# Cached K turned in 32x32 blocks on VectorE, scores a batch at a time with 32x32 tiles, and other places for the pages of K and V

## What is computed

```python
def moba_sample(q, k_new, v_new, cache_k, cache_v, page_table, layer):
    k_past = cache_k[layer, page_table].reshape(B, past, H, HD)
    kmean = jnp.mean(k_past.reshape(B, n_full, MOBA_BLOCK, H, HD), axis=2)
    idx, ok = moba_select(q, kmean, n_full)            # the 3 best of 8 blocks of 256 tokens
    s_sel = einsum('bqhd,bhqnkd->bhqnk', q, k_sel) * scale
    s_own = einsum('bqhd,bkhd->bhqk', q, k_own) * scale, causal
    return sparse_softmax_attend(s_sel, v_sel, s_own, v_own)
```

## Time and profile before

| | before |
|---|---|
| runs (us) | 977.66, 979.59, 980.74; median 979.59 |
| profiled execution, its own time | 983.45 us |
| its span | 981.3 us |
| TensorE busy / weight load | 919.1 us (94%) / 798.8 us |
| VectorE, ScalarE, GpSimd busy | 545.9, 359.5, 28.1 us |
| attention over the cache | from 446 to 670 us of the span |
| DMA | 199.93 MB, mean 204 GB/s |

### The profile page before, as it was taken

One profiled execution on the slowest core, in us unless ns is written; L12 is line 12 of the kernel. 1 busy time (PEld: TensorE's weight loads), 2 busy tenths in 40 slices (PEclk: granted clock), 3 DMA queues, 4 the chain that ended last, 5 costly groups with the idle time before them and its releaser, 6 DMA issues.

```text
span 981.3 us, 17319 instructions
## 1 busy us (share of the span) xinstructions
PE 919.1 (94%) x6991; PEld 798.8 (81%) x6991; DVE 545.9 (56%) x839; ACT 359.5 (37%) x509; POOL 28.1 (3%) x34
## 2 busy tenths in 40 slices
PE   6999999999999899999878999859899999989997
PEld 2588888988999599996665877548779999989994
DVE  0545444454655677785843538443666765554655
ACT  1424322232442534454642426240333232323433
POOL 0000000000000000000000000001200000000000
PEclk9999999998999999999999889877999999999999
DMA  9899889886456744448858998996416465534511
GB/s 329 258 299 258 240 244 257 245 235 169 127 152 191 256 129 145 144 153 268 297 190 325 324 325 310 356 343 199 125 39 167 133 163 139 145 89 122 155 50 53
DMA packets 214885, 199.93 MB, mean 204 GB/s; under 512 B 9569, under 2 KB 161261, under 8 KB 214678
## 3 DMA queue, kind: packets, MB, share of 16 engines
q1 hardware_dynamic: 213412, 194.99, 64.8%
q0 software_dynamic: 704, 2.49, 0.7%
q10 hardware_dynamic: 690, 1.35, 0.4%
HBM read 195.00 MB, written 3.80 MB: 203 GB/s over the span
## 4 chain that ended last, share of the span: by engine, by line
PE 83%; DVE 6%; ACT 3%; SPq 3%; issue 2%; DMA 2%; ACTq 0%; DVEq 0%
PE B L691 20%; PE B L692 19%; PE B L696 19%; PE B L751 4%; PE B L887 3%; PE B L898 2%; SPq L619 2%; PE B L936 2%; PE B L775 2%; PE B L760 2%; PE B L791 2%; DMA ring<-in_cache_v 1%; PE B L1017 1%; PE B L717 1%; PE B L712 1%
## 5 line engine op out<-in xcount | busy, mean ns | idle before, releaser
L691 PE MATMUL B<-Hh,wh 128*128 128x320 f32 x912 | 274.2, 314 | 0.6 <-issue 0.6
L692 PE MATMUL B<-Hl,wh 128*128 128x320 f32 x912 | 270.5, 310 | 0.0
L1595 DVE TENSOR_TENSOR wl<-raw,wh 128x2048 fp32r<-128x2048 f32 x90 | 207.3, 2305 | 94.3 <-ACT wh L1240 94.0
L1240 ACT ACTIVATE wh<-raw 128x2048 fp32r<-128x2048 f32 x90 | 172.3, 1914 | 150.3 <-PE B L696 117.6
L691 PEld LDWEIGHTS B<-Hh,wh 128*128 128x128 f32 x912 | 172.4, 189 | 10.7 <-issue 10.0
L692 PEld LDWEIGHTS B<-Hl,wh 128*128 128x128 f32 x912 | 172.4, 189 | 0.3
L696 PE MATMUL B<-Hh,wl 128*128 128x320 f32 x912 | 152.8, 310 | 0.0
L696 PEld LDWEIGHTS B<-Hh,wl 128*128 128x128 f32 x912 | 139.1, 189 | 0.0
L691 PE MATMUL B<-Gh,wh 128*128 128x320 f32 x352 | 107.1, 317 | 2.5 <-DVE Gl L1721 2.5
L692 PE MATMUL B<-Gl,wh 128*128 128x320 f32 x352 | 106.7, 316 | 0.0
L1240 ACT ACTIVATE sg<-B 128x320 f32<-128x320 f32 x46 | 20.1, 438 | 210.1 <-PE B L696 195.7
(11 more groups left out here) (246 smaller groups left out, 951.8 us busy)
## 6 DMA issues: line engine op xcount, KB each, us to landing
raw<-in_w_ffn_in SPq DMA_DIRECT2D x88, 512.0 KB, 6.2
raw<-in_w_ada SPq DMA_DIRECT2D x72, 512.0 KB, 4.9
ring<-in_cache_k SPq DMA_DIRECT2D x108, 256.0 KB, 5.3
ring<-in_cache_v SPq DMA_DIRECT2D x84, 256.0 KB, 5.0
raw<-in_w_ffn_out SPq DMA_DIRECT2D x32, 384.0 KB, 3.6
raw<-in_w_mix_in SPq DMA_DIRECT2D x24, 512.0 KB, 4.7
raw<-in_w_ffn_out SPq DMA_DIRECT2D x32, 320.0 KB, 4.3
M<-in_cache_v SPq DMA_DIRECT2D x16, 256.0 KB, 4.5
```

The lines of the kernel that those rows point to most:

```text
L691: pe.matmul(out, w, xh[k], start=start and k == 0, stop=False)
L692: pe.matmul(out, w, xl[k], start=False, stop=False)
L1240: return act.activation(out, in_, func, **kw)
L1595: dve.tensor_tensor(wl[:, wbuf(n), :], raw_view(n), f32(wh[:, wbuf(n), :]), ALU.subtract).then_inc(lo_ready, 1)
```

## The change

- **K.** A group of K is turned in place on VectorE: `dve.transpose` over 128 x 2048 turns each block of 32x32 (`turn_keys` moves from TensorE to VectorE; 4 a batch, counted by `k_turned`). The TensorE transposes, `kT`, `keys_act` and `keys_dve` go.
- **Scores.** `scores(i, bi)` handles a batch: for each x (of four blocks of 32 features within a head pair), row group a (32 token rows) and head pair c a matmul with 32 partitions, 32 output rows and 512 columns (16 pages x 32), into S4[32c.., a, :], four banks where B0 to B3 were. x sums up, and so do the two samples. `s_out` counts once a batch.
- **Queries.** `turn_queries` copies each batch's `Qz` on TensorE into the four row groups (16 matmuls with 32 columns of the identity), `queries_out` on ScalarE puts them in `Qs`. The first two stand behind slot 7 of the projection. `Qz` moves into constants that are dead by then; its clearing and filling come later.
- **Reading scores.** `scores_out` reads 256 columns (a block) an instruction, reordering them, and its accumulator gives the block's sum (`gate`): 8 instructions a pair after the second batch. `block_max` takes maxima from `prob` in two instructions.
- **Order.** `values(i, 1)` and `pick_heads(i)` run in pair i + 1's part, before its probabilities are turned. All of `probs_act` is ScalarE's. Pieces of `mix` stand at points 0 to 14, four points a pair; mix(13) before the probabilities of pair 1 are turned, mix(14) and mix(18) between `values(i, 0)` and `scores(i + 1, 0)`.
- **Places.** Eight places lie in `ring` (now over raw, wh and wl). K(0, first batch) has 0 to 3, K(0, second) 4 to 7 (6 and 7 are `prob` and `PT` afterwards), every later batch of K 0 to 3. V has 4, 5 and `IN_H`, from pair 1 on one in M; without `IN_H` from pair 2; for the last pair also 0 to 3, two more in M and one in W. V of pair 0 goes to IN_H, 4, 5, IN_H again. SP waits for `s_out` of the whole batch before it loads over K.
- **Queue order.** K(0) both batches, one V group; then for each pair K(i + 1, 0), V(i, 0), K(i + 1, 1), V(i, 1). MO and MO + 1, both now into W, before the sixth and the fourth last group.
- `BANK` hands out banks 5 to 7; OB becomes bank 4.

```diff
-GROUPS = RING // 4
+GROUPS = 8
...
-AT_POINT = {0: 0, 1: 1, 3: 2, 4: 3, 5: 4, 6: 5, 8: 6, 9: 12, 10: 13, 11: 14, 13: 15, 14: 16, 15: 17, 16: 18, 18: 19}
+AT_POINT = {x: x if x <= 6 else x + 5 for x in range(15)}
...
+PAGE_GROUPS = key_groups(0, 0) + key_groups(0, 1) + value_groups(0, 0)[:1]
+for _i in range(NPAIR):
     if _i + 1 < NPAIR:
-        PAGE_GROUPS += [("k", _i + 1, 2, bi) for bi in range(2)]
-    PAGE_GROUPS += [("v", _i, g, 1) for g in range(4)]
...
+        PAGE_GROUPS += key_groups(_i + 1, 0)
+    PAGE_GROUPS += value_groups(_i, 0)[1 if _i == 0 else 0:]
     if _i + 1 < NPAIR:
...
+        PAGE_GROUPS += key_groups(_i + 1, 1)
+    PAGE_GROUPS += value_groups(_i, 1)
...
+    for n, (kind, i, g, bi) in enumerate(PAGE_GROUPS):
+        if kind == "k":
+            b = g + 4 if (i, bi) == (0, 1) else g
+        else:
+            open_ = [b for b in FIRST_IN if FIRST_IN[b] <= n <= LAST_IN.get(b, n)]
+            b = min(open_, key=lambda b: USE_AT[PAGE_GROUPS[last[b]]] if b in last else -1)
...
                 if kind == "k":
-                    sp.wait_ge(tp_filled, FILL_AT[("k", i, g, bi, 3)] + 1)
+                    sp.wait_ge(s_out, batch(i, bi) + 1)
...
+                elif b >= 4:
+                    sp.wait_ge(used, [n for n in (MI + 10, MI + 11) if wbuf(n) == b % 2][0] + 1)
...
+            def turn_queries(i, bi):
+
+                bank = turn_bank(("q", i, bi))
+                if i == 0:
+                    pe.wait_ge(q_ready, 4)
+                for x in range(4):
+                    for q in range(4):
+                        m = pe.matmul(bank[32 * q:32 * q + 32, P * x:P * (x + 1)], ident[:, 32 * x:32 * x + 32],
+                                      Qz[:, 2 * i + bi, :, :].rearrange("p c r -> p (c r)"), start=True, stop=True)
+                m.then_inc(tp_filled, 1)
+
+            def scores(i, bi):
+
+                if bi == 0 and i >= 1:
+                    pe.wait_ge(s_act, 2 * i)
+                wait_act(("q", i, bi))
+                pe.wait_ge(k_turned, 4 * batch(i, bi) + 4)
+                b = min(BUF[GROUP_AT[("k", i, g, bi)]] for g in range(4))
+                for x in range(4):
+                    for a in range(4):
+                        for c in range(HP):
+                            f = P * c + 32 * x
+                            m = pe.matmul(S4[32 * c:32 * c + 32, a, :].rearrange("r (p j) -> r p j", p=NPAGE),
+                                          Qs[32 * a:32 * a + 32, bi, x, c, :],
+                                          ring[32 * a:32 * a + 32, 4 * b:4 * b + NPAGE, f:f + 32],
+                                          start=(bi == 0 and x == 0), stop=(bi == 1 and x == 3))
+                m.then_inc(s_out, 1)
...
             for i in range(NPAIR):
-                m0 = 5 * i + 3
+                m0 = 4 * i + 3
+                point(m0)
+                if i:
+                    values(i - 1, 1)
+                    pick_heads(i - 1)
+                point(m0 + 1)
+                turn_probs(i)
+                values(i, 0)
                 if i + 1 < NPAIR:
...
+                    point(m0 + 2)
+                    scores(i + 1, 0)
+                    if i + 2 < NPAIR:
+                        turn_queries(i + 2, 0)
+                    point(m0 + 3)
+                    own_scores(i + 1)
+                    scores(i + 1, 1)
+                    if i + 2 < NPAIR:
+                        turn_queries(i + 2, 1)
+            values(NPAIR - 1, 1)
+            pick_heads(NPAIR - 1)
...
+                for m in range(4):
+                    n = 4 * s + m
+                    last = act_(prob[:, BLK * n:BLK * (n + 1)].rearrange("p (q a j) -> p a q j", q=2, a=4),
+                                S4[:, :, 64 * n:64 * n + 64].rearrange("p a (q j) -> p a q j", q=2),
+                                accum_out=gate[:, n:n + 1])
+                last.then_inc(s_act, 1)
...
+            def turn_keys(i, bi, lo, hi):
+
+                for key in key_groups(i, bi)[lo:hi]:
+                    n = GROUP_AT[key]
+                    b = BUF[n]
+                    dve.wait_ge(page_landed[b], 64 * TURN_IN[n])
+                    v = ring[:, 4 * b:4 * b + 4, :].rearrange("p j f -> p (j f)")
+                    dve.transpose(out=v, in_=v).then_inc(k_turned, 1)
...
+                if n >= 10:
+                    turn_keys(0, 0, 2 * (n - 10), 2 * (n - 10) + 2)
...
+            turn_keys(0, 1, 0, 2)
+            own(0)
             point(1)
...
+            turn_keys(0, 1, 2, 4)
             for i in range(NPAIR):
-                m0 = 5 * i + 3
...
+                m0 = 4 * i + 3
+                block_max(i, 0)
+                block_max(i, 1)
+                choose(i)
+                if i == 0:
+                    point(2)
+                point(m0)
+                if i:
+                    own_heads(i - 1)
                     out_low(i - 1)
                 if i + 1 < NPAIR:
...
+                    turn_keys(i + 1, 0, 0, 2)
+                point(m0 + 1)
                 if i + 1 < NPAIR:
...
+                    turn_keys(i + 1, 0, 2, 4)
+                totals(i)
+                probs_dve(i, 4)
+                if i + 1 < NPAIR:
                     point(m0 + 2)
...
                     point(m0 + 3)
...
+                    own(i + 1)
+                    turn_keys(i + 1, 1, 0, 4)
```

More of the change, by code:

```diff
@@ L135, in mix_fills, with key_groups, value_groups, batch @@
     return fills
-def key_fills(i, j):
-    return [("k", i, j, bi, p) for bi in range(2) for p in range(4)]
-PAGE_GROUPS = [("k", 0, j, bi) for j in range(4) for bi in range(2)]
+def key_groups(i, bi):
+    return [("k", i, g, bi) for g in ((2, 3, 0, 1) if i == 0 and bi == 0 else range(4))]
+def value_groups(i, bi):
+    return [("v", i, g, bi) for g in range(4)]
+def batch(i, bi):
+    return 2 * i + bi
 GAPS = [[] for _ in range(12)]
@@ L151 @@
     GAPS[6 + _lv] += mix_fills(7 + _lv)
+GAPS[7] += [("q", 0, bi) for bi in range(2)]
 GAPS[8] += [("nv", t) for t in range(3)]
@@ L166 @@
 for _i in range(NPAIR):
-    _m = 5 * _i + 3
-    if _i + 1 < NPAIR:
[L169 to L173, removed]
+    _m = 4 * _i + 3
+    FILLS += point_fills(_m)
+    if _i:
+        USE += value_groups(_i - 1, 1)
+        FILLS += [("pick", _i - 1)]
+    FILLS += point_fills(_m + 1) + [("p", _i, q) for q in range(5)]
@@ L184 @@
+    PAGE_GROUPS += value_groups(_i, 1)
 GROUP_AT = {key: n for n, key in enumerate(PAGE_GROUPS)}
+USE_AT = {key: n for n, key in enumerate(USE)}
 FILL_AT = {key: n for n, key in enumerate(FILLS)}
-IN_RING, IN_H, IN_M, IN_W = range(GROUPS), GROUPS, GROUPS + 1, GROUPS + 2
-BEGIN_AT = {GROUP_AT[("v", 1, 0, 0)]: IN_M, GROUP_AT[("v", 2, 0, 0)]: IN_W}
-LAST_IN = {IN_H: GROUP_AT[("v", 2, 3, 0)], IN_M: GROUP_AT[("k", 3, 3, 1)], IN_W: GROUP_AT[("v", 3, 0, 0)]}
-def place_groups():
[L193 to L199, removed]
+IN_H, IN_M, IN_M1, IN_M2, IN_W2 = range(GROUPS, GROUPS + 5)
@@ L266, in shape_constants @@
     parts["cos"], parts["sin"] = cos, sin
+    reset = np.ones((P, N))
+    reset[:, [0] + [S + T * b for b in range(NB)]] = 0.0
+    parts["reset"] = reset
     q = p[:, None]
@@ L1360, in probs_act @@
             def probs_act(i):
-                for q in (2, 3):
+                for q in range(4):
                     wait_fill(("p", i, q))
@@ L1480, in _ @@
                     level_exps(1)
+                if n == 7:
+                    queries_out(0, 0)
+                    queries_out(0, 1)
                 if n == 8:
@@ L1548, in _ @@
+            for b in (4, 5):
+                _, vi, vg, vb = PAGE_GROUPS[LAST_GROUP[b]]
+                act.wait_ge(v_used, v_index(vi, vb, vg) + 1)
+                high(At(MO + b - 4))
+            out_high(NPAIR - 1)
             for k in range(4):
@@ L2142, in _ @@
+            low(At(MO))
+            own_heads(NPAIR - 1)
+            out_low(NPAIR - 1)
+            low(At(MO + 1))
             dve.wait_ge(stored, STORED_MIX * 16)
```

315 lines of the change are left out of this document (94 added, 221 removed).

## The result

The changed kernel takes 1042.05 us (median, 1038.04 to 1051.06), the kernel before 980.13 beside it: ratio 1.0642, 95% interval 1.0595 to 1.0689, so 62 us more. A repeat in another series gave 1.0635 (1.058 to 1.069). I had predicted 1001.0, in the range 968 to 1034: slower as forecast, but by three times as much. The profiled execution took 1044.89 us, its span is 1042.9.

The account below looks back on a forecast made before the run. The in-order load queue bounds the cache attention: transfers plus rests, 63 us replacing 45. Projection start 678.9, plus 1.8, 2.7 and 8.0, gives 691.4 against 670.0: +21.4 on 979.6, so 1001.0 us, range 968 to 1034.

Parts of the forecast that it names:

- No change: Rival: half the faster case's savings hidden, or turns at their low bound and the clock holds; 983 to 984 us, chance 0.11.
- the faster first pair: Rival: VectorE and ScalarE steps overlap, so the first pair's rests of 9.6 and 16.9 go; 966.5 us, chance 0.20.
- slow turns: Rival: VectorE's turn of a K group is slower than its landing; 1015 us at 3.3 each, 1039 at twice; chance 0.08.
- the tile rival: Rival: row tiles share TensorE's array in the scores; 42, 57 or 120 ns a record give 1015, 1031, 1092; chance 0.11.
- The sum of the queue's walk: Attention over the cache: 168.0 us of transfers plus 63.0 of queue rests put the last V at 674.1 us.
- the allowances of 12.5 us: Added after the walk: 1.8 us for turning queries, 2.7 for loading out_gla_sample, 8.0 for TensorE's clock.
- (b): Scores on TensorE: 128 records of 32x32 tiles at 28 ns, 3.6 us a batch, 29 in all.
- (d): VectorE's 32 turns of K groups: 2.3 us each, below the 2.7 us in which a group lands.
- K(i+1, second batch) waits for scores(i+1, first): Load queue: K reuses four places, so once a pair it rests until scores end; 9.4, 16.0 and 9.1 us.
- the rival in which these three rests vanish: K takes other places, so rests before its second batches go, 34.5 us; 966.5 us, chance shared with the 0.20 faster case.
- In a batch only the last turn shows: VectorE's turns, 2.3 us each, hide behind the 2.7 us landings of K groups, except a batch's last.
- The allowance of 8 us for the clock: TensorE idles before five score batches and restarts at a lower clock: 1.6 us each, 8.0 in all.

Follow-up runs that it names:

- e9: Changed kernel with the next pair's first scores moved between the third and fourth group of values(i, first half) on TensorE; 1016.55 us, ratio 1.0361.
- e1: Changed kernel with the next pair's first scores moved before values(i, first half) on TensorE; 1039.15 us, ratio 1.0609.
- e2: Changed kernel with unread products added on TensorE before five score batches (18, 45, 52) to keep its clock up; 1065.16 us, ratio 1.0842.
- e5: Changed kernel with fewer unread products added before five score batches (11, 27, 30) to keep TensorE's clock up; 1040.26 us, ratio 1.0611.
- e15: Same kernel as e5, measured again in more rounds; 1041.49 us, ratio 1.0626.

## Why the prediction was wrong, point by point

**Right.** The bound is the queue, and its rests make the time: +61.5 us of rests for +62. The turn, 2.3 us forecast, 2.297 measured; the Trainium skill's rate ("Vector Engine (DVE) Microarchitecture Reference", § 3.8), one element per cycle and lane, gave an estimate of some 2.1, a little under the 2.297 of the trace. The transposes saved on TensorE show nowhere in the time, though no run takes them alone. In this stage SP waits longest at the score line (71.6 us), and before each second batch TensorE waits 13 to 18 us for turns, where I had 10 to 13. No change, the faster first pair and slow turns are excluded; of the tile rival, whose mildest form had 42 ns a record, half is true (35 ns).

**The sum of the queue's walk.** My checkpoints (without the allowances of 12.5 us that I added at the end) against the trace; those that the prediction doesn't print follow from its rests at 2.71 us a group, to within 1 us:

| | forecast | trace | behind | added since the line above |
|---|---|---|---|---|
| scores(0,0) done | 455.9 | 459.6 | 3.7 | 3.7 |
| scores(0,1) done | 476.5 | 483.0 | 6.5 | 2.8 |
| fourth V group issued | 498.9 | 509.9 | 11.0 | 4.5 |
| scores(1,0) done | 510.8 | 524.3 | 13.5 | 2.5 |
| scores(1,1) done | 529.2 | 547.8 | 18.6 | 5.1 |
| scores(2,0) done | 570.5 | 597.7 | 27.2 | 8.6 |
| scores(2,1) done | 588.8 | 622.5 | 33.7 | 6.5 |
| scores(3,0) done | 622.9 | 664.5 | 41.6 | 7.9 |
| scores(3,1) done | 641.4 | 691.1 | 49.7 | 8.1 |
| last V landed | 674.1 | 728.2 | 54.1 | 4.4 |

The same by rests: for my 9.6, 16.9, 9.4, 1.2, 16.0 and 9.1 us the trace has 10.7, 20.6, 11.9, 4.7, 23.0 and 14.1, and 5.5 for the 0.8 at the start. Two rests for which the sum has no term (3.2 and 4.6, before the fourth V groups of pair 2) and 14.3 us in short ones come on top. No single step is to blame; four terms were short at every turn of the loop:

1. *(b) Scores, 18.5 us, of which I had allowed 8.* At full clock a batch takes 4.46 us and not 3.6: 35 ns a record of 32x32 tiles with 512 columns, where I had carried over 27 to 28 ns from 128 columns. That is 0.86 x 8 = 6.9 us; the other 11.6 (47.3 - 35.7) are the clock, on all batches but one. My readings of the rows were also low: 64 records in 1.96 us are 30.6 ns each by plain division (3.9 us a batch), and 16 in 1.16 us are 72.5 and not 60. The Trainium skill's 10.6 for 16 tiles ("TensorE: Matmul & The Clock Gate", Part 3) had pointed to an estimate of 5.4 us; the measured 4.46 lies between it and mine.
2. *The way from K's issue to its scores, 10.3 us.* I gave 1.2 to 1.3 us to the start of the bytes, 2.71 a group and one turn (14.4; 14.8 between the checkpoints). It took 17.0, 17.8 and 19.9 (issued 524.49, 597.83, 664.70; scores from 541.50, 615.67, 684.61). The first K(1,1) is the example: its last group lands at 539.04, 14.5 us after the issue, not 12.1. Behind the rest the queue comes up slowly: 72, 209 and 252 GB/s in the stretches of 1 us from 525 on, and 389 in the fourth. The bare rate of a queue that never rests also leaves out the scattered slack, the rests of under 1 us, which the kernel before has too: 18.4 of its 51.0 us (14.3 of 112.5 after). I had counted only the long ones. The three issues in SP's timeline:

```profile
524.49 9.68 SPq L643 DMA_DIRECT2D ring<-in_cache_k  x16
...
597.83 9.97 SPq L643 DMA_DIRECT2D ring<-in_cache_k  x16
...
664.70 11.08 SPq L643 DMA_DIRECT2D ring<-in_cache_k  x16
```

3. *(d) Turns in front of VectorE's other work, 8.8 us.* My sum has no term for K(1,0)'s and K(3,0)'s turns. The chain of waits of the changed kernel, of 480 to 530 us and of 545 to 665 (start us, us, what):

```profile
484.00 2.04 ACT ring L1254 x11
486.07 1.23 DVE small L1786
...
500.37 4.41 DVE ring L1781 x2
504.78 0.32 DVE Hl L1875
505.14 3.42 PE B L949 x16
...
511.88 3.44 DMA pages_l<-in_cache_v
515.37 1.93 PE B L967 x32
...
635.80 4.41 DVE ring L1781 x2
640.71 0.62 DVE W L1959 x2
...
643.03 1.97 PE B L949 x8
```

Two turns stand in front of a prompt step at 500 us and in front of the states at 636, 4.4 us each. A fourth V group waits for its place here in pair 2 as well (issued at 647.28, a rest of 3.2); my walk had that in pair 0 alone.
4. *Low clock on the rest of the path, and the fourth V groups of the second halves.* The rests before these are 4.7 us in pair 0 and 4.6 in pair 2, for 1.2 and none; from the landing of V(1, first half) to scores(2,0) it is 13.5 us for 11.1. On the chain eight L1084 records take 3.7 us at 655 where eight take 2.0 at 623 with the clock up, and V's 32 products 1.93 for 1.06. With smaller slips this is what is left of the 54: some 17 us, which I haven't taken apart by runs.

**Which step the runs overthrow.** "K(i+1, second batch) waits for scores(i+1, first)" is right as a wait, and issuing these groups earlier is worth the 28 us of e9. But the rival in which these three rests vanish (34.5 us off) took K's places as the only ones that bind; e1 put these scores early and got 3 us, since V's fourth groups and K(3,0) then waited. "In a batch only the last turn shows" is wrong: by the no-change rival I had nine turns on the path, 20.7 us, and leaving out all gave 31; the chain holds these nine and the four of point 3 (8.8 us), 29.1 in all. The allowance of 8 us for the clock was short of the 11.6 that the batches show, but the runs that took 5.9 of them back gained 2 to 3, so the clock under the scores isn't where most of the missing 40 us lie. As to the range: its upper end took each slow rival alone, with the rest of the sum fixed, and no case in which all terms are a little short together, which is what happened.

## What to carry to other kernels

When a buffer is freed by a batch and no longer by a piece, everything between the landing and the release (turn, product, idle engine, other work queued in front) is paid once a batch by the transfer queue; price each step on that path by its slowest row, and add the slack that the old trace shows beside its long rests. Before an order is changed to end one wait, ask which place the next transfer in the queue needs: moving the scores ahead of the values gained 3 us, within the noise; moving them into the wait behind the third group gained 28 us. Where a sum has a dozen terms of one sign of uncertainty, the range has to hold the case that all are short.

## What the runs showed of the hardware that I had not expected

- 16 float32 products of 32x32 tiles with 512 columns: 35 ns a record at full clock (128 records in 4.46 us), 46 to 53 ns in batches that begin at the lower clock level (5.92 to 6.79 us). Tiles of 128x32 take 120 ns a record with as many columns (16 records in 1.92 us).
- Added products kept the granted clock at 1.00 from 447 to 490 us in e2, and in the whole profiled execution it rose from 0.904 to 0.938 in e5; e5's time hardly followed, and e2's rose, for the added products outran their gap.
- In e5 and e15 TensorE stalls at the same instruction, 1.65 and 1.67 us before the last record of the sixth batch, on nothing that the profile shows ("issue"). The changed kernel has no such stall there. I don't know its cause.
